# The projections of the mixing stage: plain fp32 products against three products of two-part operands

## The chip, the cores and the metric

One core of one Trainium2 chip runs the whole program: TensorE (PE in the profile) multiplies matrices, ScalarE (ACT), VectorE (DVE) and GpSimd (POOL) do the rest, and SyncE (SP) issues the weight loads. The metric is the time of one execution on the device in microseconds. The kernel before takes 1591.19 us, the median of three runs (1590.81 to 1591.87).

## The reference

Two transformer blocks on a sequence of 256 tokens with 1024 features, all in fp32. The change is in the mixing stage of the first block, behind its first feed-forward part:

```python
u = rms_norm(h, norm_mix)
proj = u @ w_in                       # [256 x 1024] @ [1024 x 4864]
aq, ak, av, rq, rf, ri, rg, ga, gb = jnp.split(proj, splits, axis=-1)
att = sliding_window_attention(aq, ak, av, rel_bias, attn_sinks)   # 8 heads of 64, window of 128
rec = hgrn2_recurrence(rq, rf, ri, lower_bounds)                   # 4 heads of 128
rec = rms_norm(rec, rec_norm) * sigmoid(rg)
merged = sigmoid(ga) * (att @ w_att_proj) + sigmoid(gb) * (rec @ w_rec_proj)
h = h + merged @ w_out
```

Only how `u @ w_in` is computed changes, and with it where its operands are kept.

## The kernel before

**Layout.** The features of `h` and of the scaled input `xT` lie on the partitions in eight tiles of 128, the 256 tokens along the row. `w_in` is cut into 19 chunks of 256 columns, 1 MB each. In the order of use they are `rf` (0, 1), `rq` (0, 1), `ri` (0, 1), `aq` (0, 1), `akv`, `rg` (0, 1) and `g` (0 to 7); below they are counted as chunks 0 to 18. All weights of the program pass through six bays of 1 MB. SyncE loads a chunk into its bay as soon as TensorE has used the chunk that lay there six places before (`load`, line 656).

**Products.** A chunk costs 16 matmuls of 128 x 128 by 128 x 256 (eight tiles of input features by two halves of the chunk), by `pair_of_features` (line 894, matmuls in `features`, line 808) or, for `ri`, `pair_of_tokens` (line 907). Plain fp32 matmuls stand in the trace as two records each. In `akv` the first half (keys) goes by features and the second (values) by tokens, with matmuls of 128 columns (line 975). The feed-forward parts already work in another way: ScalarE rounds a chunk into a first part in fp32r (line 1489), VectorE subtracts it from the raw chunk and writes the second part (line 2053), the input is split likewise, and TensorE sums first by first, second by first and first by second (`split_features`, lines 828 to 832): 48 matmuls to a chunk, each one record.

**Order.** Each engine runs its own list in the order in which it is written, and semaphores hold an instruction until what it needs is there. Around the change:
- TensorE (`mix1`, line 947): the embedding's product in four pieces (line 792), between them the sum of squares (line 744), the table of attention biases by distance (line 953) and the spread of the norm factors (line 780). Then chunks 0 to 10, the attention scores of eight heads (lines 991, 992), and a loop of nine steps over the levels of the recurrence: the level's scores (line 1013), then one of chunks 11 to 18.
- VectorE (line 2130): before the stage it adds the feed-forward result to `h` (line 2019) and folds squares (line 1983). Then it writes `xT` (line 2038), copies the bias table (line 2520), moves products out of PSUM, adds the biases to the scores (line 2160), and at each level multiplies (2190, 2191) and places masked scores (2184); behind level 3 it scales the probabilities (2232).
- ScalarE (line 1536): squares (1465), the embedding out of PSUM (1590), then `bias_out`: it issues a DMA that writes the bias table, copied 128 times, from eight partitions to a buffer in HBM (1534, 1.5 MB). After keeping `rf` it waits until that has landed and issues two loads that read it back shifted (1541, 1542). Then it keeps products (`keep`, line 1526) and takes exponentials (1557, 1561).
- GpSimd forms the differences of each level (1858, 1859).

## Time and profile before

| | |
|---|---|
| median of three runs | 1591.19 us |
| profiled execution | 1592.14 us, its span 1590.4 us |
| TensorE busy | 1499.5 us, 94% |
| VectorE, ScalarE, GpSimd busy | 832.7, 558.9, 152.0 us |
| mean granted TensorE clock | 0.956 of full speed |

The span runs from the first instruction to the last. The clock is the share of 2.4 GHz that TensorE was granted. The profile's times count from the span's start; the mixing stage runs from about 216 to 459 us, its projections from 227 to 385 us.

### The profile page before, as it was taken

How to read it: one execution, taken by the hardware profiler on the slowest of the kernel's cores; microseconds unless marked ns; L12 is line 12 of the kernel's file. 1: busy time of each engine (PE TensorE's matmuls, PEld its weight loads, DVE VectorE, ACT ScalarE, POOL GpSimd, SP SyncE). 2: the span in 40 equal slices, each digit the busy share in tenths (PEclk: the TensorE clock that was granted, in tenths of full speed). 3: DMA queues.
4: the chain of work that ended last, by engine and by line, in shares of the span. 5: the costliest groups of instructions: out<-in, count | busy, mean ns of one | idle time of the engine just before them, and what ended most of it. 6: DMA issues, size and time to landing. Idle time of an engine off the chain costs nothing.

```text
span 1590.4 us, 24781 instructions
## 1 busy us (share of the span) xinstructions
PE 1499.5 (94%) x10432; PEld 1398.4 (88%) x10432; DVE 832.7 (52%) x1130; ACT 558.9 (35%) x689; POOL 152.0 (10%) x149
## 2 busy tenths in 40 slices
PE   5999999899999999999979998999989889999997
PEld 5999998798899999988878878999988468999997
DVE  4666541253256565632664215766674263776765
ACT  3434321123035454421335103443442154444443
POOL 0000000121000000511020000000050032000023
PEclk8999999999999999999989759999999999999998
DMA  8555557533345555433400014455543312455530
GB/s 270 191 185 185 184 153 187 165 106 106 106 159 175 184 183 188 155 99 118 137 25 1 1 53 133 161 184 184 185 159 103 133 53 74 165 185 184 185 133 27
DMA packets 167213, 221.31 MB, mean 139 GB/s; under 512 B 5451, under 2 KB 148036, under 8 KB 167012
## 3 DMA queue, kind: packets, MB, share of 16 engines
q1 hardware_dynamic: 163564, 216.46, 41.2%
q10 hardware_dynamic: 3576, 3.81, 1.3%
q8 instruction: 55, 0.90, 0.2%
q14 instruction: 18, 0.15, 0.0%
HBM read 217.49 MB, written 2.62 MB: 138 GB/s over the span
## 4 chain that ended last, share of the span: by engine, by line
PE 85%; DVE 7%; ACT 4%; issue 2%; POOL 1%; DMA 0%; ACTq 0%; POOLq 0%; SPq 0%; DVEq 0%
PE ps L832 30%; PE ps L868 14%; PE ps L808 12%; PE ps L936 6%; PE ps L918 2%; PE ps L907 2%; PE ps L1231 1%; PE ps L792 1%; DVE x_second_part L1973 1%; PE ps L1352 1%; PE ps L818 1%; PE ps L1368 1%; PE ps L1013 1%; PE ps L1226 1%; PE ps L1380 1%
## 5 line engine op out<-in xcount | busy, mean ns | idle before, releaser
L2053 DVE TENSOR_TENSOR weights_second_parts<-weight_bays,weights_first_parts 128x2048 fp32r<-128x2048 f32 x132 | 302.9, 2302 | 173.5 <-ACT weights_first_parts L1489 173.2
L1489 ACT ACTIVATE weights_first_parts<-weight_bays 128x2048 fp32r<-128x2048 f32 x132 | 252.1, 1918 | 302.8 <-PE ps L832 191.4
L832 PE MATMUL ps<-x_first_part,weights_first_parts 128*128 128x256 f32 x1488 | 211.2, 285 | 1.7 <-DVE weights_second_parts L2053 1.7
L832 PE MATMUL ps<-x_second_part,weights_first_parts 128*128 128x256 f32 x1488 | 208.6, 283 | 0.0
L832 PE MATMUL ps<-x_first_part,weights_second_parts 128*128 128x256 f32 x1488 | 207.3, 282 | 0.0
L808 PE MATMUL ps<-xT,weight_bays 128*128 128x256 f32 (+1 forms) x896 | 197.4, 381 | 1.1 <-DVE xT L2038 1.1
L832 PEld LDWEIGHTS ps<-x_first_part,weights_first_parts 128*128 128x128 f32 x1488 | 192.6, 193 | 2.1 <-ACT weights_first_parts L1489 1.9
L832 PEld LDWEIGHTS ps<-x_second_part,weights_first_parts 128*128 128x128 f32 x1488 | 191.7, 191 | 0.0
L808 PEld LDWEIGHTS ps<-xT,weight_bays 128*128 128x128 f32 (+1 forms) x896 | 168.5, 189 | 26.1 <-ACT embedding L1597 1.3
L832 PEld LDWEIGHTS ps<-x_first_part,weights_second_parts 128*128 128x128 f32 x1488 | 190.6, 191 | 0.0
L868 PE MATMUL ps<-hidden_first_part,weights_first_parts 128*128 128x256 f32 x704 | 141.9, 283 | 5.4 <-ACT weights_first_parts L1489 3.7
L868 PE MATMUL ps<-hidden_second_part,weights_first_parts 128*128 128x256 f32 x704 | 141.9, 283 | 0.0
L868 PE MATMUL ps<-hidden_first_part,weights_second_parts 128*128 128x256 f32 x704 | 139.7, 279 | 0.0
L1868 POOL TENSOR_TENSOR weights_second_parts<-weight_bays,weights_first_parts 128x512 fp32r<-128x512 f32 x48 | 66.7, 1422 | 535.1 <-ACT weights_first_parts L1607 535.1
L868 PEld LDWEIGHTS ps<-hidden_first_part,weights_first_parts 128*128 128x128 f32 x704 | 107.7, 189 | 6.1 <-ACT weights_first_parts L1489 4.0
L868 PEld LDWEIGHTS ps<-hidden_second_part,weights_first_parts 128*128 128x128 f32 x704 | 109.1, 190 | 0.0
L868 PEld LDWEIGHTS ps<-hidden_first_part,weights_second_parts 128*128 128x128 f32 x704 | 108.8, 189 | 0.0
L936 PE MATMUL ps<-arena,weight_bays 128*128 128x256 f32 x320 | 71.6, 386 | 6.5 <-DVE arena L2406 4.5
L936 PEld LDWEIGHTS ps<-arena,weight_bays 128*128 128x128 f32 x320 | 61.7, 194 | 16.0 <-DVE arena L2406 4.7
L1842 POOL TENSOR_TENSOR rstd<-mean_squares,minus_half 128x2 f32<-128x2 f32 (+3 forms) x16 | 14.9, 934 | 562.5 <-DVE mean_squares L2025 426.2
L1526 ACT ACTIVATE arena<-ps 128x512 f32<-128x512 f32 x14 | 8.4, 597 | 121.5 <-PE ps L808 95.0
L1505 ACT ACTIVATE arena<-arena 128x512 f32<-128x512 f32 x22 | 13.9, 633 | 99.9 <-DVE arena L2072 99.9
(369 smaller groups left out, 1882.6 us busy)
## 6 DMA issues: line engine op xcount, KB each, us to landing
weight_bays<-in_w_ffn_in SPq DMA_DIRECT2D x44, 1024.0 KB, 5.2
weight_bays<-in_ffn_w_in SPq DMA_DIRECT2D x44, 1024.0 KB, 5.1
weight_bays<-in_w_ffn_out SPq DMA_DIRECT2D x22, 1024.0 KB, 4.9
weight_bays<-in_ffn_w_out SPq DMA_DIRECT2D x22, 1024.0 KB, 4.9
weight_bays<-in_w_in SPq DMA_DIRECT2D x19, 1024.0 KB, 5.5
weight_bays<-in_hyb_w_in SPq DMA_DIRECT2D x13, 1024.0 KB, 5.2
weight_bays<-in_ple_w_gate SPq DMA_DIRECT2D x8, 1024.0 KB, 4.9
weight_bays<-in_w_out SPq DMA_DIRECT2D x4, 1024.0 KB, 5.0
```

Of the source, the lines that this page charges most:

```text
L792: mm = nc.tensor.matmul(ps[:, b0 + q, j % 2 * SEQ:(j % 2 + 1) * SEQ], w[:, k, j * P:(j + 1) * P], pT[:, n, k], start=(k == 0), stop=(k == 1))
L808: mm = nc.tensor.matmul(dst, lhs(k), xT[:, k] if rhs is None else rhs(k), start=(k == 0), stop=(k == n - 1), **kw)
L818: nc.tensor.matmul(dst[j], w[:, k, j * P:(j + 1) * P], x_hi[:, k], start=(k == 0 and w is hi and not (one_bank and j)), stop=False, skip_g ...
L832: mm = nc.tensor.matmul(dst, w[:, k, j * P:(j + 1) * P], x[:, k], start=(n + k == 0), stop=(n == 2 and k == KD - 1))
L868: mm = nc.tensor.matmul(ps[:, tile // 2, tile % 2 * SEQ:(tile % 2 + 1) * SEQ], w[:, j, tile * P:(tile + 1) * P], x[:, g % 2, j], start=(g ...
L907: mm = nc.tensor.matmul(ps[:, b, t * width:(t + 1) * width], xT[:, k, t * P:(t + 1) * P], w[:, k, c0:c0 + width], start=(k == 0), stop=(k ...
L918: mm = nc.tensor.matmul(ps[:, b0 + j // 2, j % 2 * SEQ:(j % 2 + 1) * SEQ], w[k // 2][:, k % 2, j * P:(j + 1) * P], srcT[:, k], start=(k == ...
L936: mm = nc.tensor.matmul(ps[:, tile // 2, tile % 2 * SEQ:(tile % 2 + 1) * SEQ], w[:, j, tile * P:(tile + 1) * P], srcT(k) if callable(srcT) ...
L1013: mm = nc.tensor.matmul(o, a, c, start=True, stop=True)
L1489: nc.scalar.activation(hi, raw, ACT.Copy).then_inc(*w_hi_ready.inc(f, g, kind, of - g))
L1868: ins = nc.gpsimd.tensor_tensor(lo[:, part], raw[:, part], hi[:, part], ALU.subtract)
L2053: v.tensor_tensor(lo, raw, hi, ALU.subtract).then_inc(*w_lo_d.inc(f, g, kind, of - g))
```

## The change

Every chunk of `w_in` is split as in the feed-forward parts. ScalarE writes the first part (`prep`), VectorE the second (`rest_of_mix`), and TensorE runs 48 matmuls on them (`mix_features`, `mix_tokens`). First parts go to three slots in turn, and from chunk 13 on to two others (`late_hi`) in the place of the bias rows. The scaled input goes to the buffer `sq`, from there as first parts by ScalarE to `xT`'s place and as second parts by VectorE back into `sq`. All of `akv` goes by features now, and the values are turned by two transposes of TensorE. GpSimd's clearing of `AT` waits for the input's second parts.

```diff
+        mixer_lo = nc.alloc_sbuf_tensor_at("mixer_x_second_part", [P, KD, SEQ], F32R, offset=nc.sbuf_base - 4 * KD * SEQ)
         xT = sb("xT", [P, KD, SEQ])
+        mixer_hi = nc.alloc_sbuf_tensor_at("mixer_x_first_part", [P, KD, SEQ], F32R, offset=nc.sbuf_base - 4 * KD * SEQ)
...
+        late_hi, _ = carve_split(ARENA - 2 * BAY, "gate_weights_first_parts", 2, BAY)
...
+        MIX_SLOT = [n % 3 for n in range(12)] + [1]
+
+        def mix_views(m):
+
+            c = chunks[MIX_CHUNKS[m]] % BAYS
+            hi = w_hi[:, MIX_SLOT[m]] if m < len(MIX_SLOT) else late_hi[:, (m - len(MIX_SLOT)) % 2]
+            return [t.rearrange("p (a b) -> p a b", a=KD) for t in (bay[:, c], hi, bay_lo[:, c])]
...
+            mixer_x = (mixer_hi, mixer_lo)
+
+            def wait_mix(m):
+                pe.wait_ge(*w_hi_ready.at(MIX_CHUNKS[m]))
+                pe.wait_ge(*w_lo_d.at(MIX_CHUNKS[m]))
+                return mix_views(m)[1:]
+
+            def mix_features(m, b):
+
+                hi, lo = wait_mix(m)
+                if m == 0:
+                    mm = first_features("mix1", [ps[:, b, j * SEQ:(j + 1) * SEQ] for j in range(2)], hi, lo, True, mixer_x)
+                else:
+                    for j in range(2):
+                        mm = split_features(ps[:, b, j * SEQ:(j + 1) * SEQ], hi, lo, j, mixer_x)
+                through(mm, MIX_CHUNKS[m])
+            def mix_tokens(m, b):
+
+                hi, lo = wait_mix(m)
+                for t in range(TT):
+                    for n, (x, w) in enumerate(((mixer_hi, hi), (mixer_lo, hi), (mixer_hi, lo))):
+                        for k in range(KD):
+                            mm = nc.tensor.matmul(ps[:, b, t * SEQ:(t + 1) * SEQ], x[:, k, t * P:(t + 1) * P], w[:, k],
+                                                  start=(n + k == 0), stop=(n == 2 and k == KD - 1))
+                through(mm, MIX_CHUNKS[m])
...
-                pair_of_features(("rf", 0), 0, first="mix1")
-                pair_of_features(("rf", 1), 1)
-                pair_of_features(("rq", 0), 2)
+                mix_features(0, 0)
+                mix_features(1, 1)
+                mix_features(2, 2)
                 pe.wait_ge(*bias_d.at("t"))
-                pair_of_features(("rq", 1), 3)
+                mix_features(3, 3)
                 for n in range(2):
-                    weights(("ri", n))
                     pe.wait_ge(*proj_a.at("rf", n))
-                    through(pair_of_tokens(("ri", n), n), ("ri", n))
+                    mix_tokens(4 + n, n)
                 for n in range(2):
                     pe.wait_ge(*proj_d.at("rq", n))
-                    pair_of_features(("aq", n), 2 + n)
-                weights("akv")
+                    mix_features(6 + n, 2 + n)
                 pe.wait_ge(*proj_a.at("ri", 0))
...
+                mix_features(8, 0)
+                pe.wait_ge(*proj_a.at("ri", 1))
+                mix_features(9, 1)
+                pe.wait_ge(*proj_d.at("aq", 0))
+                mix_features(10, 2)
+
+                pe.wait_ge(*proj_d.at("akv"))
...
                 for t in range(TT):
+                    mm = nc.tensor.transpose(ps[:, 0, t * P:(t + 1) * P], vT[:, t * P:(t + 1) * P], ident)
+                mm.then_inc(*att_p.inc("v_turned"))
...
-                        pair_of_features(("g", n), pb)
+                        mix_features(11 + n, pb)
...
+            def prep(m):
+                raw, hi, _ = mix_views(m)
+                wait_weights(act, MIX_CHUNKS[m])
+                if m < 3:
+                    act.wait_ge(*used_up_to(("ffn1", 3 * GROUPS - 3 + m)))
+                elif m < len(MIX_SLOT):
+                    act.wait_ge(*used_up_to(MIX_CHUNKS[m - (3 if m < 12 else 2)]))
+                elif m < len(MIX_SLOT) + 2:
+                    act.wait_ge(*att_d.at("biased", AH - 1))
+                else:
+                    act.wait_ge(*used_up_to(MIX_CHUNKS[m - 2]))
+                nc.scalar.activation(hi, raw, ACT.Copy).then_inc(*w_hi_ready.inc(MIX_CHUNKS[m]))
+
             def mix1():
+                for q in range(PAIRS):
+                    act.wait_ge(*x_d.at("mix1", q))
+                    nc.scalar.activation(mixer_hi[:, 2 * q:2 * q + 2], sq[:, 2 * q:2 * q + 2], ACT.Copy).then_inc(*x_hi_a.inc("mix1", q))
+                bias_out()
                 for n in range(2):
+                    prep(2 + n)
                     keep(fT[:, 2 * n:2 * n + 2], n, ("rf", n), "rf", n, func=ACT.Sigmoid)
                 act.wait_ge(tab_out.sem, 16)
                 shifted = [bass.AP(tensor=scratch.tensor, offset=127 + o, ap=[[383, P], [384 * P, AH], [1, n]]) for o, n in ((0, 256), (P, P))]
                 act.dma_start(bias[:, :, 0:256], shifted[0]).then_inc(bias_in.sem, 16)
                 act.dma_start(bias[:, :, 256:384], shifted[1]).then_inc(bias_in.sem, 16)
+                prep(4)
+                prep(5)
                 for n in range(2):
+                    prep(6 + n)
                     keep(vR[:, :, n * 256:(n + 1) * 256], n, ("ri", n), "ri", n)
                 act.wait_ge(*rec_d.at("f"))
                 nc.scalar.activation(bT[:], fT[:], ACT.Ln).then_inc(*rec_a.inc("log"))
+                prep(8)
+                prep(9)
+                prep(10)
...
                 for n in range(2):
+                    prep(11 + n)
                     keep(sgT[:, 2 * n:2 * n + 2], 1 + n, ("rg", n), "rg", n)
 
                 act.wait_ge(*att_d.at("minus_max"))
...
                     act.wait_ge(*rec_g.at("differences", n))
                     nc.scalar.activation(zT[:, n % 2], zT[:, n % 2], ACT.Exp).then_inc(*rec_a.inc("decay", n))
                     keep(gT[:, 2 * n:2 * n + 2], (3 + n) % 4, ("g", n), "g", n)
+                    if n < 6:
+                        prep(13 + n)
...
+            prep(0)
+            prep(1)
             arrive("mix1")
             embedding("ple1", 4)
-            bias_out()
             mix1()
...
-                pool.wait_ge(*mean_ready.at("mix1"))
-                pool.wait_ge(*bias_p.at("t"))
+                pool.wait_ge(*x_lo_d.at("mix1", PAIRS - 1))
...
+            def rest_of_mix(m):
+                raw, hi, lo = mix_views(m)
+                dve.wait_ge(*w_hi_ready.at(MIX_CHUNKS[m]))
+                v.tensor_tensor(lo, raw, hi, ALU.subtract).then_inc(*w_lo_d.inc(MIX_CHUNKS[m]))
+
+            def split_x(n, gain, b):
+                dve.wait_ge(*spread_p.at(n))
+                for k in range(KD):
+                    ins = v.scalar_tensor_tensor(sq[:, k], h[:, k], gain(k), ps[:, b, 0:SEQ], ALU.mult, ALU.mult)
+                    if k % 2:
+                        ins.then_inc(*x_d.inc(n, k // 2))
+                for q in range(PAIRS):
+                    p = slice(2 * q, 2 * q + 2)
+                    dve.wait_ge(*x_hi_a.at(n, q))
+                    v.tensor_tensor(mixer_lo[:, p], sq[:, p], mixer_hi[:, p], ALU.subtract).then_inc(*x_lo_d.inc(n, q))
...
                 dve.wait_ge(*masks_ready.at())
                 for n in range(2):
+                    rest_of_mix(2 + n)
                     dve.wait_ge(*proj_a.at("rf", n))
                     if n == 0:
                         dve.wait_ge(*lb_d.at("one_minus"))
...
                 for n in range(2):
+                    rest_of_mix(4 + n)
                     keep(rqT[:, 2 * n:2 * n + 2], 2 + n, ("rq", n), "rq", n)
                 dve.wait_ge(*rec_d.at("f"))
                 v.tensor_scalar(kT[:], fT[:], -1.0, 1.0, ALU.mult, ALU.add).then_inc(*rec_d.inc("q_and_k"))
+                rest_of_mix(6)
+                rest_of_mix(7)
...
                 for n in range(2):
+                    rest_of_mix(8 + n)
                     keep(aqT[:, 2 * n:2 * n + 2], 2 + n, ("aq", n), "aq", n, scale=0.125)
                 dve.wait_ge(*rec_d.at("scan"))
                 v.tensor_copy(bT[:], fT[:]).then_inc(*rec_d.inc("sums"))
+                rest_of_mix(10)
                 dve.wait_ge(*used_up_to("akv"))
                 v.tensor_copy(akT[:, 0], ps[:, 0, 0:SEQ]).then_inc(*proj_d.inc("akT"))
...
-                keep(av[:], 0, "akv", "akv", c=slice(256, 512))
+                v.tensor_copy(vT, ps[:, 0, SEQ:2 * SEQ]).then_inc(*proj_d.inc("akv"))
+                rest_of_mix(11)
+                dve.wait_ge(*att_p.at("v_turned"))
+                v.tensor_copy(av[:], ps[:, 0, 0:SEQ].rearrange("p (a b) -> p a b", a=TT)).then_inc(*proj_d.inc("av"))
...
+                rest_of_mix(12)
...
                         normalize_probs()
+                    if n < 6:
+                        rest_of_mix(13 + n)
...
+            rest_of_mix(0)
+            rest_of_mix(1)
             arrive("mix1", added("ffn1", 0.5, ("ffn1", 3 * GROUPS - 1)))
             factors("mix1", b=0)
-            scaled_x("mix1", lambda k: col("norm_mix", k), 1)
+            split_x("mix1", lambda k: col("norm_mix", k), 1)
```

Three places show what this does to the order.

**ScalarE, from the last piece of the embedding to chunk 5.** L1534 is the write of the bias table, L1541 and L1542 the two loads that read it back, L1526 keeps a product. Before:

```order
L1590 ACTIVATE embedding<-ps 128x512 [waits weights_used]
L1530 ACTIVATE lower_bound<-lower_bound_logit 128x4 [waits lower_bound_by_vector]
L1534 DMA bias_by_distance<-arena 1024x1x384 [waits bias_by_distance_copied]
L1526 ACTIVATE arena<-ps 128x512 [waits weights_used] x2
L1541 DMA arena<-bias_by_distance 128x8x256 [waits bias_by_distance_stored]
L1542 DMA arena<-bias_by_distance 128x8x128
L1526 ACTIVATE arena<-ps 128x2x256 [waits weights_used] x2
```

Now (L1571, L1596, L1597 are the same three DMAs, L1563 keeps a product, L1584 writes the first part of a chunk, L1589 that of the input):

```order
L1654 ACTIVATE embedding<-ps 128x512 [waits weights_used]
L1589 ACTIVATE mixer_x_first_part<-squares 128x512 [waits xT_by_vector] x4
L1567 ACTIVATE lower_bound<-lower_bound_logit 128x4 [waits lower_bound_by_vector]
L1571 DMA bias_by_distance<-arena 1024x1x384 [waits bias_by_distance_copied]
L1584 ACTIVATE weights_first_parts<-weight_bays 128x2048 [waits weights_used,weights_landed0]
L1563 ACTIVATE arena<-ps 128x512 [waits weights_used]
L1584 ACTIVATE weights_first_parts<-weight_bays 128x2048 [waits weights_used,weights_landed1]
L1563 ACTIVATE arena<-ps 128x512 [waits weights_used]
L1596 DMA arena<-bias_by_distance 128x8x256 [waits bias_by_distance_stored]
L1597 DMA arena<-bias_by_distance 128x8x128
L1584 ACTIVATE weights_first_parts<-weight_bays 128x2048 [waits weights_used,weights_landed2]
L1584 ACTIVATE weights_first_parts<-weight_bays 128x2048 [waits weights_used,weights_landed3]
```

Four input parts stand ahead of the write, the first parts of chunks 2 and 3 ahead of the two loads, and the first parts of chunks 4 and 5 behind them.

**VectorE, at the end of the feed-forward part.** L2019 adds the result to `h`, L1983 folds squares. Before:

```order
L1968 TENSOR_TENSOR one_and_squared_gain<-vector_columns 128x8
L2019 SCALAR_TENSOR_TENSOR h<-ps,h 128x512 [waits projection_ready] x3
L2019 SCALAR_TENSOR_TENSOR h<-ps,h 128x512 [waits weights_used]
L1983 TENSOR_TENSOR squares<-squares 128x512 [waits squares_summed]
L1983 TENSOR_TENSOR squares<-squares 128x512 [waits vector_step,squares_summed]
L2025 TENSOR_SCALAR mean_squares<-ps 128x2 [waits squares_added]
```

Now, with L2109 as the second part of a weight chunk, L2083 and L2047 for L2019 and L1983:

```order
L2032 TENSOR_TENSOR one_and_squared_gain<-vector_columns 128x8
L2109 TENSOR_TENSOR weights_second_parts<-weight_bays,weights_first_parts 128x2048 [waits weights_first_part_ready] x2
L2083 SCALAR_TENSOR_TENSOR h<-ps,h 128x512 [waits projection_ready] x3
L2083 SCALAR_TENSOR_TENSOR h<-ps,h 128x512 [waits weights_used]
L2047 TENSOR_TENSOR squares<-squares 128x512 [waits squares_summed]
L2047 TENSOR_TENSOR squares<-squares 128x512 [waits vector_step,squares_summed]
L2089 TENSOR_SCALAR mean_squares<-ps 128x2 [waits squares_added]
```

The second parts of chunks 0 and 1 stand ahead of the four updates of `h`.

**VectorE, two levels of the recurrence.** L2190 and L2191 multiply, L2184 places scores under a mask. Before:

```order
L2190 TENSOR_TENSOR arena<-arena 128x256x2 [waits recurrence_by_scalar]
L2191 TENSOR_TENSOR arena<-arena 128x256x2
L2184 COPY_PREDICATED arena<-masks,ps 128x512 [waits recurrence_by_vector,recurrence_by_tensor]
L2184 COPY_PREDICATED arena<-masks,ps 128x512
L2190 TENSOR_TENSOR arena<-arena 128x128x4 [waits recurrence_by_scalar]
L2191 TENSOR_TENSOR arena<-arena 128x128x4
L2184 COPY_PREDICATED arena<-masks,ps 128x512 [waits recurrence_by_vector,recurrence_by_tensor]
L2184 COPY_PREDICATED arena<-masks,ps 128x512
```

Now (L2280, L2281 and L2274 are the same three lines):

```order
L2109 TENSOR_TENSOR weights_second_parts<-weight_bays,gate_weights_first_parts 128x2048 [waits weights_first_part_ready]
L2280 TENSOR_TENSOR arena<-arena 128x256x2 [waits recurrence_by_scalar]
L2281 TENSOR_TENSOR arena<-arena 128x256x2
L2274 COPY_PREDICATED arena<-masks,ps 128x512 [waits recurrence_by_vector,recurrence_by_tensor]
L2274 COPY_PREDICATED arena<-masks,ps 128x512
L2109 TENSOR_TENSOR weights_second_parts<-weight_bays,gate_weights_first_parts 128x2048 [waits weights_first_part_ready]
L2280 TENSOR_TENSOR arena<-arena 128x128x4 [waits recurrence_by_scalar]
L2281 TENSOR_TENSOR arena<-arena 128x128x4
L2274 COPY_PREDICATED arena<-masks,ps 128x512 [waits recurrence_by_vector,recurrence_by_tensor]
L2274 COPY_PREDICATED arena<-masks,ps 128x512
L2109 TENSOR_TENSOR weights_second_parts<-weight_bays,gate_weights_first_parts 128x2048 [waits weights_first_part_ready]
```

Before each level's two products now stands the second part of a gate chunk.

## Rows read from the trace of the kernel before

**Rows 1.** The page, part 1: busy us (share) and instructions of each engine
```profile
PE 1499.5 (94%) x10432; PEld 1398.4 (88%) x10432; DVE 832.7 (52%) x1130; ACT 558.9 (35%) x689; POOL 152.0 (10%) x149
```

**Rows 2.** The chain of waits in order of time: start us, us, what
```profile
54.79 11.40 PE ps L832 x96
...
219.27 1.68 PE ps L744 x16
...
227.45 27.63 PE ps L808 x128
255.08 13.81 PE ps L907 x64
268.89 17.27 PE ps L808 x80
286.16 3.57 PE ps L975 x32
...
316.68 7.70 PE ps L808 x32
324.38 1.78 PE ps L1013 x16
```

**Rows 3.** The page, part 5: splitting a chunk; busy us, mean ns of one, idle before
```profile
L2053 DVE TENSOR_TENSOR weights_second_parts<-weight_bays,weights_first_parts 128x2048 fp32r<-128x2048 f32 x132 | 302.9, 2302 | 173.5 <-ACT weights_first_parts L1489 173.2
L1489 ACT ACTIVATE weights_first_parts<-weight_bays 128x2048 fp32r<-128x2048 f32 x132 | 252.1, 1918 | 302.8 <-PE ps L832 191.4
```

**Rows 4.** Timeline of ScalarE, stage entry: start us, us, instruction, idle before it
```profile
209.74 1.08 ACT L1782 ACTIVATE pT<-ps 128x512 f32<-128x512 f32 x2 [3.32 <-PE ps L729]
...
227.49 0.60 ACT L1590 ACTIVATE embedding<-ps 128x512 f32<-128x512 f32 x1 [2.37 <-PE ps L792]
...
229.16 0.84 ACTq L1534 DMA_DIRECT2D bias_by_distance<-arena  x1
...
264.69 0.42 ACTq L1541 DMA_DIRECT2D arena<-bias_by_distance  x1
...
265.78 0.60 ACT L1526 ACTIVATE arena<-ps 128x512 f32<-128x512 f32 x1 [23.88 <-issue]
```

**Rows 5.** Timeline of VectorE, stage entry
```profile
215.85 0.69 DVE L2019 SCALAR_TENSOR_TENSOR h<-ps,h 128x512 f32<-128x512 f32 x1 [0.72 <-PE ps L868]
216.46 1.48 DVE L1983 TENSOR_TENSOR squares<-squares 128x512 f32<-128x512 f32 x2
...
228.59 0.54 DVE L2520 COPY arena<-ps 8x384 f32<-8x384 f32 x1
```

**Rows 6.** DMA queues, 243 to 246 us (two rows), then 246 to 249 us (two rows)
```profile
q1 hardware_dynamic: 499, 0.50, 48.6%
q10 hardware_dynamic: 93, 0.14, 45.1%
...
q10 hardware_dynamic: 94, 0.14, 45.6%
q1 hardware_dynamic: 1, 0.00, 0.0%
```

**Rows 7.** Busy time by stretch: PE, PEld, DVE, ACT, POOL, PEclk, DMA share, GB/s
```profile
312.90:318.10 5.20, 5.20 (x20) 4.92 (x21) 1.11 (x5) 3.95 (x18) 0.00 (x0) 0.50 0.02 3
```

**Rows 8.** Timeline, the recurrence's levels: VectorE and GpSimd
```profile
322.96 0.69 DVE L2191 TENSOR_TENSOR arena<-arena 128x512 f32<-128x512 f32 x1
...
326.60 1.53 DVE L2191 TENSOR_TENSOR arena<-arena 128x512 f32<-128x512 f32 x1
328.05 1.33 DVE L2184 COPY_PREDICATED arena<-masks,ps 128x512 f32<-128x512 uint8 x2
...
347.14 3.76 DVE L2232 TENSOR_SCALAR arena<-arena,softmax_sum 128x256 f32<-128x256 f32 x16
...
326.24 1.33 POOL L1858 TENSOR_TENSOR arena<-arena 128x512 f32<-128x512 f32 x1 [38.09 <-PE ps L1013]
```

**Rows 9.** Timeline of ScalarE, an exponential of the recurrence
```profile
324.91 1.05 ACT L1561 ACTIVATE arena<-arena 128x1024 f32<-128x1024 f32 x1
```

More of the change, by code:

```diff
@@ L389, in build @@
         sgT, at = carve(at, RH, SEQ)
+        akT, at = carve(at, 2, SEQ)
         gT, at = carve(at, 16, SEQ)
@@ L438, in build @@
         block_out = signal("first_block_out")
+        MIX_CHUNKS = [("rf", 0), ("rf", 1), ("rq", 0), ("rq", 1), ("ri", 0), ("ri", 1), ("aq", 0), ("aq", 1), "akv", ("rg", 0), ("rg", 1),
+                      *[("g", n) for n in range(8)]]
+        MIX_SLOT = [n % 3 for n in range(12)] + [1]
[3 more added lines that the diff above has]
+            return [t.rearrange("p (a b) -> p a b", a=KD) for t in (bay[:, c], hi, bay_lo[:, c])]
         def ple_views(key):
@@ L809, in features, with first_features @@
                 return mm
-            def first_features(f, dst, hi, lo, one_bank):
+            def first_features(f, dst, hi, lo, one_bank, xs=(x_hi, x_lo)):
                 for q in range(PAIRS):
@@ L1019, in mix1 @@
                         elif n == 1:
-                            pe.wait_ge(*proj_d.at("akv"))
+                            pe.wait_ge(*proj_d.at("av"))
                         elif n < 4:
```

20 lines of the change are left out of this document (5 added, 15 removed).

## The prediction

> **What bounds the kernel now.** I read the page first. TensorE is busy for 94% of the span [rows 1], so what its own work costs counts nearly in full, unless something new makes it wait. The chain of waits in order of time comes next: from 227.45 us on it holds nothing but projection matmuls, one chunk behind the other, until the attention scores [rows 2]. VectorE and ScalarE have idle time there. So the question is in two parts: what a chunk costs TensorE in either form, and whether the two helpers deliver the parts in time. For the second I read the timelines of ScalarE and VectorE from the end of the feed-forward part on, each against the new order of instructions.
>
> **A chunk on TensorE.** Plain fp32: 27.63 us for 128 records, which are four chunks, so 6.91 us each. Two-part: 11.40 us for 96 matmuls of the same shape, which are two chunks of the feed-forward part, so 5.70 us each [rows 2]. That is 1.21 us less per chunk. `akv` costs 3.57 us for the values and two tenths of the 17.27 us for half a chunk by features (80 records are five halves, 3.45 each), 7.02 in all; now 5.70, 1.32 less. The two transposes of the values add 0.5 us (a level's 16 records of 128 columns take 1.78 us [rows 2], four such records 0.45). With TensorE never waiting, 18 x 1.21 + 1.32 - 0.5 = 22.6 us would be gained.
>
> **Stage entry.** ScalarE is done with `pT` at 209.74 + 1.08 = 210.82 [rows 4] and now writes two first parts, 1.92 us each [rows 3]: 212.74 and 214.66. VectorE's second parts take 2.30 each [rows 3] and end at 215.04 and 217.34. Only then come the four updates of `h`, the last of which started at 215.85 before. They follow each other at 0.61 us (215.85 to 216.46 [rows 5]), so the last starts at 219.2, the squares at 219.8 and end 1.48 later, at 221.2. TensorE began the sum at 219.27 [rows 2]: it is 1.9 us late, and so is the end of the embedding, 229.4 instead of 227.45. ScalarE then takes the last piece of the embedding out of PSUM (0.60 [rows 4]) before it rounds the first pair of `x`, a copy of the same size. TensorE starts chunk 0 at 230.6 and is done with chunk 3 at 230.6 + 4 x 5.70 = 253.4 us. The parts of chunks 2 and 3 are there by then: each needs 4.2 us of the two helpers, and TensorE has work for 11.4 us before chunk 2.
>
> **The wait for the bias table.** This decides. In the new order ScalarE writes the first parts of chunks 4 and 5 only behind the two loads of the bias, and these wait until the table's write to HBM has landed. Before, the write was issued at 229.16 and ScalarE got past that wait at 264.69, 35.5 us later [rows 4]. It cost nothing then: behind it stood only the keeping of `ri`, done at 261.99, and TensorE went on with raw chunks. Now TensorE needs chunk 4's parts. The write itself is issued later: the four copies of `x` end at 232.4, VectorE's last second part takes about 0.7 us (to 233.1), the copy of the table 0.54 [rows 5] with a small one ahead of it, so the write starts at 233.8. I keep 35.5 us for it: 269.3. The two loads are issued within 1.1 us (264.69 to 265.78 [rows 4]), the first part takes 1.92, the second 2.30: chunk 4 starts at 274.6, where it started at 255.08 [rows 2]. TensorE stands for 21.2 us and is **19.5 us late**. VectorE is in the same jam: its second part of chunk 4 stands ahead of `rq`'s keeping, which chunk 6 waits for, but it has 11 us for that..
>
> **From there to the end of the stage** come 15 chunks, 14 x 1.21 + 1.32 = **-18.3 us**, and the transposes, **+0.5**. In these 15 the helpers mostly keep up. A gate round costs TensorE 1.78 + 5.70 = 7.48 us. ScalarE has 0.60 + 1.92 + 1.05 in it [rows 3, 4, 9]. VectorE has the second part 2.30, two products (0.69 each, one of them 1.53 while GpSimd works) and the placing 1.33 [rows 3, 8]: 5.0 to 5.9. Two places are tight. The first level's products ended at 323.65 [rows 8], 0.7 us ahead of the end of the gate chunk at 324.38 [rows 2], which now comes 1.2 earlier: 0.5 us of wait. And behind level 3 VectorE has the 3.8 us of the probabilities [rows 8] in one round, 9.2 to 9.6 in all against 7.48, of which about 1.5 is slack: 0.4 us more. Together **+0.9**; the bounds are 0 and 4.
>
> **The clock.** After TensorE stood for 3.5 us ahead of 312.89, its granted clock was 0.50 for the next 5.2 us, the 1.2 GHz level [rows 7], and a chunk there took 7.70 us instead of 6.91 [rows 2]. Half of 5.2 is 2.6 us. The new wait of 21 us is longer than that one, and I price what follows it the same, **+2.6**. It can be no gain; the bounds are 0 and twice the row, 5.2. The old wait ahead of the first level stays and is counted already.
>
> **Sum.** 19.5 - 18.3 + 0.5 + 0.9 + 2.6 = +5.2 us on the profiled execution's 1592.14 us (span 1590.4 and 1.7 around it), 1597.3. That execution lay 0.95 above the median of the runs, so I forecast 1596 for the median, with some tenths off for instructions that overlap by 0.08 where I added full durations. Behind the stage nothing changes: later loads have room, since TensorE's wait only fills the bays.
>
> **The rule on the write.** The rows: in 243 to 246 us the write (q10) moved 93 packets beside 499 of the weight loads (q1), in 246 to 249 it moved 94 beside one [rows 6], both at 45% of the 16 DMA engines. So its speed doesn't depend on the weight loads, and the long stop of these doesn't shorten it. The Trainium skill, "DMA: Bandwidth & Descriptors", section "Why a DMA increments its semaphore by 16 and not by 1", says that a DMA uses the largest number of engines up to 16 that divides the outer sizes of both sides. The write reads eight partitions: eight engines, and 45% agrees. The same page, "Queues, rings and completion order", has each engine take turns between the queues that have work. By that rule the write would get the engines whole once TensorE stops and no load is left; the trace disagrees. It is the ground of the first rival.
>
> **Rivals.**
> - *Faster, the write lands earlier.* Place: ScalarE's wait for the table. If the weight loads did share the write's engines and their stop halved its 35.5 us, it would land at 251.6. Chunk 4 would start at 256.9, 1.8 us late instead of 19.5, with a short wait and no cold clock: 1596 - 17.7 - 2.6 = 1576. The change gains from the point where the write is over 5 us shorter, and by over 0.2% from 8.4 us. For it: loads and write do run side by side. Against it: rows 6, and that few loads are under way in the write's second half already. 12%, all shortenings together.
> - *No difference.* The wait is as forecast, but the clock comes back sooner or the entry and the gate rounds lose nothing: 19.5 - 18.3 + 0.5 + 1 = +2.7, 1594. 20%.
> - *VectorE bounds the gate rounds.* GpSimd's differences run beside it, and a product of 0.69 took 1.53 meanwhile [rows 8]. If the second parts stretched in the same proportion, 2.30 to 5.1, a round would be 8.7 us against TensorE's 7.48, and six rounds would lose 1.2 each: 1603. Against it: the stalled product lost 0.84 us, about what was left of one GpSimd instruction of 1.33, which looks like waiting once and not like half speed. The Trainium skill, "GPSIMD Engine Reference", "Specifications", says that the two engines contend where VectorE reads two inputs from SBUF, as the second parts do; it gives no price. 8%.
> - *The two-part chunks don't cost 5.70.* The input's parts lie elsewhere and `ri` has them as the stationary side, but shape and type are those of the row. If they cost 6.3, 15 x 0.6 = 9 us more, 1605. 2%.
>
> **Chances and range.** The forecast holds 58%. What a measurement can tell from no change is 0.2%, 3.2 us, so faster is below 1588 and slower above 1594.4. Faster 0.12, same 0.20, slower 0.68 (58 + 8 + 2). The forecast's own range is 1594.5 to 1601. With the second rival and part of the third it is 1590 to 1602; the faster case is left out.
>
> **What would show it.** ScalarE: idle for about 27 us ahead of the first load of the bias, at 269. TensorE: one idle stretch of about 21 us behind the fourth chunk, ended by the second part of chunk 4, with the granted clock at 0.50 for some microseconds behind it; 48 matmuls in 5.70 us everywhere else; gate rounds of 7.5 us. The level scores behind the last gate chunk at 390 us instead of 385. Wrong it would be if ScalarE passed the wait before 260, if TensorE's stretch were under 15 us, or if gate rounds took 8 us or more.

## The result, and the profile after

The changed kernel takes 1599.9 us, the median of 14 runs (1595.4 to 1602.44); the kernel before, run beside it on the same chips, 1588.11 (14 runs, 1584.38 to 1592.24). The ratio is 1.0063, with a 95% interval of 1.0049 to 1.0077: slower, by 8 to 12 us. The profiled execution took 1596.38 us, its span 1594.4.

The executions of either kernel fall mostly into two groups some 6 us apart (the kernel before: seven of 1584.38 to 1585.41 us and seven of 1590.81 to 1592.24, with the median between them), and since the profiled execution of before (1592.14) is of the upper group and that of after (1596.38) by its time of the lower, the 4 us between their spans are not the cost of the change. The cost is read from the ratio, and from the stage itself. From the start of the embedding's product to the start of the attention's output projection it took 402.23 - 215.65 = 186.58 us before and 412.00 - 215.10 = 196.90 after: +10.3 us, in line with the ratio (0.63% of 1588 is 10.0). All stage times below are read this way. A second execution of the kernel before (experiment 9) has 184.68, which would make it +12.2: stages of single executions can be compared to within some 2 us, and what a smaller difference means has to be read from the rows.

The page, part 1, answers to [rows 1]:

```profile
PE 1476.2 (93%) x10722; PEld 1388.0 (87%) x10722; DVE 877.8 (55%) x1154; ACT 595.4 (37%) x712; POOL 160.9 (10%) x149
```

TensorE is busy for 23 us less than before and the program is slower all the same: it stands more. The waits of TensorE between 215 and 412 us say where (line of the waiting matmul, what it waits for, us in total, times, longest):

```profile
PE ps L939 <- DVE weights_second_parts L2109: 21.0, 1, 21.0
PE ps L1050 <- DVE arena L2281: 4.0, 2, 2.7
PE ps L1050 <- DVE arena L2249: 3.5, 1, 3.5
PE ps L758 <- DVE squares L2047: 1.7, 1, 1.7
PE ps L1092 <- ACT arena L1644: 1.7, 1, 1.7
PE ps L832 <- ACT mixer_x_first_part L1589: 1.3, 1, 1.3
```

The third and the fifth row stood before too (3.5 and 1.7). The other four are new. The first is the forecast's main term. The chain of waits in order of time (start us, us, what), answering to [rows 2]:

```profile
220.45 2.62 PE ps L758 x16
...
234.99 35.06 DMA bias_by_distance<-arena
270.53 0.59 ACTq L1597
271.22 1.92 ACT weights_first_parts L1584
273.16 2.30 DVE weights_second_parts L2109
275.60 13.34 PE ps L939 x96
288.94 28.33 PE ps L846 x240
...
337.67 2.05 PE ps L1050 x16
339.72 5.67 PE ps L846 x48
...
370.76 2.88 PE ps L1050 x16
373.65 6.38 PE ps L846 x48
380.03 1.78 PE ps L1050 x16
381.81 5.69 PE ps L846 x48
```

The write of the bias table is now a link of the chain, 35.06 us long; where it stood beside the chain before, TensorE now waits for ScalarE's first part behind it and VectorE's second. A chunk costs 5.67 us (28.33 for five of 48 matmuls), as forecast. ScalarE's timeline answers to [rows 4]:

```profile
234.99 0.84 ACTq L1571 DMA_DIRECT2D bias_by_distance<-arena  x1
...
270.07 0.42 ACTq L1596 DMA_DIRECT2D arena<-bias_by_distance  x1
270.53 0.59 ACTq L1597 DMA_DIRECT2D arena<-bias_by_distance  x1
271.22 5.51 ACT L1584 ACTIVATE weights_first_parts<-weight_bays 128x2048 fp32r<-128x2048 f32 x3 [27.27 <-issue]
```

Between the write and the loads ScalarE is idle for the longer part, 27 us, and three first parts follow in a row behind it. The granted clock (column behind POOL) in three half-speed stretches that are new or longer than before, answering to [rows 7]:

```profile
221.50:228.30 6.80, 6.80 (x21) 4.79 (x21) 0.64 (x3) 0.11 (x1) 0.70 (x1) 0.50 0.00 0
259.10:279.60 20.50, 4.00 (x19) 4.03 (x20) 6.44 (x6) 5.51 (x3) 0.00 (x0) 0.50 0.82 220
371.70:375.10 3.40, 3.40 (x18) 3.40 (x17) 3.40 (x4) 0.00 (x0) 1.37 (x1) 0.50 0.20 80
```

Each lies in or behind one of the new waits. Before, the profiled execution had 3.4 us at half speed at the first place and none at the other two.

VectorE's timeline in the gate rounds, answering to [rows 8]:

```profile
355.33 2.74 DVE L2109 TENSOR_TENSOR weights_second_parts<-weight_bays,gate_weights_first_parts 128x2048 fp32r<-128x2048 f32 x1 [1.44 <-ACT gate_weights_first_parts L1584]
357.99 1.60 DVE L2280 TENSOR_TENSOR arena<-arena 128x512 f32<-128x512 f32 x1
...
361.82 5.39 DVE L2324 TENSOR_SCALAR arena<-arena,softmax_sum 128x256 f32<-128x256 f32 x16
```

The probabilities take 5.39 us instead of 3.76, a second part 2.74 instead of 2.30. GpSimd at the same time (its rows are rough):

```profile
354.87 1.05 POOL L1922 TENSOR_TENSOR arena<-arena 128x512 f32<-128x512 f32 x1 [3.40 <-PE ps L1050]
355.88 3.17 POOL L1923 TENSOR_TENSOR arena<-arena 128x512 f32<-128x512 f32 x1
```

### The profile page after: what moved, and what is told of

It is laid out like the page before. It is cut to its first block, busy times and chain, and to the rows that moved or that the text cites. A ratio compares the mean times of both kernels' runs of the same rounds, so it can differ in the third digit from the quotient of the medians.

```text
span 1594.4 us, 25429 instructions
## 1 busy us (share of the span) xinstructions
PE 1476.2 (93%) x10722; PEld 1388.0 (87%) x10722; DVE 877.8 (55%) x1154; ACT 595.4 (37%) x712; POOL 160.9 (10%) x149
## 4 chain that ended last, share of the span: by engine, by line
PE 79%; DVE 10%; ACT 4%; DMA 3%; issue 2%; POOL 1%; ACTq 0%; POOLq 0%; SPq 0%; DVEq 0%
PE ps L846 33%; PE ps L882 14%; PE ps L977 5%; PE ps L822 5%; DMA bias_by_distance<-arena 2%; PE ps L959 2%; PE ps L1268 1%; DVE x_second_part L2037 1%; PE ps L1389 1%; PE ps L1405 1%; PE ps L832 1%; PE ps L1263 1%; PE ps L806 1%; PE ps L948 1%; PE ps L1417 1%
## 5 line engine op out<-in xcount | busy, mean ns | idle before, releaser
L2133 DVE TENSOR_TENSOR weights_second_parts<-weight_bays,weights_first_parts 128x2048 fp32r<-128x2048 f32 x132 | 301.1, 2289 | 172.0 <-ACT weights_first_parts L1526 171.6
L1526 ACT ACTIVATE weights_first_parts<-weight_bays 128x2048 fp32r<-128x2048 f32 x132 | 252.1, 1918 | 299.5 <-PE ps L846 190.1
L822 PE MATMUL ps<-xT,weight_bays 128*128 128x256 f32 (+1 forms) x368 | 80.8, 380 | 1.1 <-DVE xT L2102 1.1
L822 PEld LDWEIGHTS ps<-xT,weight_bays 128*128 128x128 f32 (+1 forms) x368 | 68.2, 186 | 12.7 <-ACT embedding L1661 1.3
L2109 DVE TENSOR_TENSOR weights_second_parts<-weight_bays,weights_first_parts 128x2048 fp32r<-128x2048 f32 x13 | 29.9, 2307 | 42.6 <-ACT weights_first_parts L1584 42.6
L1542 ACT ACTIVATE arena<-arena 128x512 f32<-128x512 f32 x22 | 13.9, 633 | 99.9 <-DVE arena L2152 99.9
```

Of the source, the lines that this page charges most:

```text
L822: mm = nc.tensor.matmul(dst, lhs(k), xT[:, k] if rhs is None else rhs(k), start=(k == 0), stop=(k == n - 1), **kw)
L1526: nc.scalar.activation(hi, raw, ACT.Copy).then_inc(*w_hi_ready.inc(f, g, kind, of - g))
L2109: v.tensor_tensor(lo, raw, hi, ALU.subtract).then_inc(*w_lo_d.inc(MIX_CHUNKS[m]))
L2133: v.tensor_tensor(lo, raw, hi, ALU.subtract).then_inc(*w_lo_d.inc(f, g, kind, of - g))
```

## The experiments

There are nine experiments. Their stage times (before 186.6, after 196.9) come from one profiled execution each, the ratios from timed runs against the kernel before.

**1. The wait for the table behind the second `ri` piece.**

```diff
-                act.wait_ge(tab_out.sem, 16)
-                shifted = [bass.AP(tensor=scratch.tensor, offset=127 + o, ap=[[383, P], [384 * P, AH], [1, n]]) for o, n in ((0, 256), (P, P))]
-                act.dma_start(bias[:, :, 0:256], shifted[0]).then_inc(bias_in.sem, 16)
-                act.dma_start(bias[:, :, 256:384], shifted[1]).then_inc(bias_in.sem, 16)
                 prep(4)
                 prep(5)
                 for n in range(2):
                     prep(6 + n)
                     keep(vR[:, :, n * 256:(n + 1) * 256], n, ("ri", n), "ri", n)
+                act.wait_ge(tab_out.sem, 16)
...
```

> The changed kernel with ScalarE's wait for the bias table and the two loads behind it moved from ahead of the first parts of chunks 4 and 5 to behind the keeping of ri. The stage is measured from the start of the embedding's product to the start of the first output projection: 186.6 us in the kernel before, 196.9 in the changed one. Theory 1 (the write stands in ScalarE's queue and besides holds the weight loads issued while it runs): chunks 4 and 5 start without a wait at 254 and 260 us, and TensorE then stands about 8 us for chunk 6, whose load lands only with the write's end near 270 us; the stage takes 182 to 184 us, some 14 less than in the changed kernel. Rival (the loads are not held, only ScalarE's queue was): no wait of TensorE before the attention scores, the stage takes 173 to 175 us. Rival 2 (TensorE's wait had another cause): 196 to 197 us as before.

Measured: 1591.16 us, ratio 1.0007 (0.999 to 1.0024); stage 186.1. The wait ahead of chunk 4 is gone, and with it the loss: the position of that wait is what made the change slower. But 8.3 us came back ahead of chunk 6. The stage is above the 182 to 184 expected, since that wait had half clock behind it too (30.87 us for chunks 6 to 10 instead of 28.33) and the stretch at half clock in the gate rounds was 6.8 us long instead of 3.4. The chain shows from where the 8.3 us come:

```profile
237.77 32.19 DMA weight_bays<-in_w_in
...
269.98 1.92 ACT weights_first_parts L1584
...
271.92 2.31 DVE weights_second_parts L2109
...
274.36 30.87 PE ps L846 x240
```

A weight load of 1 MB, issued at 237.77 while the write of the table was under way, landed 32.19 us later, when the write was done. So the write holds up TensorE in two ways: through ScalarE's wait, and, once that is gone, through the weight loads beside it.

**2. The probabilities three rounds later.** They are wanted only behind the last gate chunk.

```diff
-                    if n == 3:
+                    if n == 6:
                         normalize_probs()
```

> The changed kernel with the scaling of the probabilities moved on VectorE from behind level 3 to behind level 6, nothing else. Theory (the scaling, 5.4 us beside GpSimd's differences, makes the products of level 4 late): TensorE's wait of 2.7 us ahead of level 5 and the 1.8 us of half clock behind it go, stage 192.0 to 193.0 us instead of 196.9. Rival (VectorE's total work per round is the bound): the wait only moves to a later level, stage above 195.5.

Measured: 1593.52 us in one run; stage 192.5, 4.4 less. The wait of 2.7 us at 370.8 is gone, and so is the half-speed stretch behind it; that at 338 stays with 1.1. The theory holds: the scaling was what made TensorE wait. Of these 4.4 us the prediction had 0.4.

**3. The table written 32 times instead of 128.** The loads then read it in four groups of 32 partitions; what arrives in the bias rows is the same.

```diff
-                act.dma_start(scratch, tabd[:].unsqueeze(1).to_broadcast([AH, P, 384])).then_inc(tab_out.sem, 16)
+                act.dma_start(scratch[:, 0:32], tabd[:].unsqueeze(1).to_broadcast([AH, 32, 384])).then_inc(tab_out.sem, 16)
...
+                for r in range(0, P, 32):
+                    for c, o, n in ((0, 0, 256), (256, P, P)):
+                        src = bass.AP(tensor=scratch.tensor, offset=127 + o - r, ap=[[383, 32], [384 * P, AH], [1, n]])
+                        act.dma_start(bias[r:r + 32, :, c:c + n], src).then_inc(bias_in.sem, 16)
```

> The changed kernel, with the bias table written to HBM 32 times instead of 128, and read back in four groups of 32 partitions (eight loads instead of two, the same bytes read and the same values). Theory (the length of the write sets the wait, 35.1 us at 128 copies): the write lands about 10 us after its issue, near 245 us; with some 4 us for issuing eight loads chunk 4's parts are ready at 254, when TensorE comes for them; its 21.0 us of waiting and the 1.9 us of half clock behind it go, the stage takes 173.5 to 175.5 us, and the kernel 21 to 23 us less than the changed one. Rival (the write's time is mostly a fixed cost of its landing, not of its bytes): the write still takes over 25 us and the gain is under 10 us. The gate rounds keep their waits of 4.0 us in sum.

Measured: 1580.75 us, ratio 0.9938 (0.9915 to 0.9962); stage 175.6. The write was issued at 234.91 and ScalarE passed the wait at 244.28, 9.4 us later. So the write's time goes with its bytes, and the rival is refuted. TensorE goes from chunk 3 to chunk 4 with no wait, and chunk 6 doesn't wait either:

```profile
249.97 4.60 PE ps L846 x39
254.58 11.52 PE ps L939 x96
266.10 28.33 PE ps L846 x240
```

With the write out of the way the stage is 11 us shorter than before, though the entry and the gate rounds still lose what they lost.

**4. The same 32 copies in the kernel before**, to see whether the write alone is worth something.

> The kernel before with the same 32 copies and eight loads, its products unchanged. Theory (the write cost nothing there, since raw chunks 4 and 5 were in their bays and ScalarE's lateness held nobody): no difference, stage 186.3 to 187.0 us, ratio within 0.2% of 1. Rival (the write's slowing of the weight loads already cost the kernel before something): 1 to 3 us faster.

Measured: 1591.09 us, ratio 0.9997 (0.998 to 1.0014); stage 186.5. The write was free there, to within what the interval leaves open. It is the change that put a price on it.

**5. The entry: the second parts of chunks 0 and 1 behind the updates of `h`.**

```diff
-            rest_of_mix(0)
-            rest_of_mix(1)
             arrive("mix1", added("ffn1", 0.5, ("ffn1", 3 * GROUPS - 1)))
+            rest_of_mix(0)
             factors("mix1", b=0)
             split_x("mix1", lambda k: col("norm_mix", k), 1)
+            rest_of_mix(1)
```

> The changed kernel with VectorE's second parts of chunks 0 and 1 behind the four updates of h (chunk 0's ahead of the norm factors, chunk 1's behind the second parts of x), nothing else. Theory (those two hold the updates of h, and with them the sum of squares, the factors, x and the write of the bias table): TensorE's wait of 1.7 us ahead of the sum goes, chunk 0 starts 2 to 5 us earlier, the write is issued as much earlier, and chunk 4, which waits for it, too: stage 192 to 195 us instead of 196.9. Rival (the entry is hidden in the 21 us of waiting): stage unchanged at 196.9, since TensorE only waits longer.

Measured: 1597.96 us in one run; stage 194.7, 2.2 less. Chunk 0 started 3.5 us earlier (228.24 instead of 231.78), but chunk 4 only 1.0 earlier, at 274.56: TensorE now stood 23.4 us ahead of it instead of 21.0. The write went out at 233.65, only 1.3 us earlier, since the second part of chunk 1 (2.28 us from 230.80 on) now stands ahead of the table's copy on VectorE. So most of what the entry gained was waited away, and of the 1.0 us another 0.4 went in chunks 4 and 5, which took 13.79 us instead of 13.34. The rival is nearly right. The rest of the 2.2 us, 1.6, lies in the gate rounds: in this execution the wait of 2.7 us, which is still there, has no stretch at half clock behind it. The edit does not touch that place, so I don't count these 1.6 us for it.

**6. All of 2, 3 and 5.**

> The changed kernel with three edits: 32 copies as in the run before; the second parts of chunks 0 and 1 behind the updates of h (one ahead of the factors, one behind the second parts of x); and the scaling of the probabilities moved from behind level 3 to behind level 6. Theory: to the 23 us of the shorter write come 1.7 us of wait and about 3 us of half clock and later start at the entry, and 2.7 us of wait and 1.8 of half clock at level 5; the stage takes 165 to 168 us, 19 to 21 us less than in the kernel before, and the whole about 1.2% less than before. Rival (VectorE's total work bounds the gate rounds, wherever the scaling stands): the 4.5 us of the gate rounds stay, stage 170 us or more.

Measured: 1574.79 us, ratio 0.9907 (0.9883 to 0.9931); stage 172.7, above the 165 to 168 expected. TensorE stood for 5.1 us ahead of chunk 4. ScalarE was past the wait at 243.2, so it wasn't the write:

```profile
243.21 8.80 ACTq L1598 DMA_DIRECT2D arena<-bias_by_distance  x8
252.12 5.51 ACT L1584 ACTIVATE weights_first_parts<-weight_bays 128x2048 fp32r<-128x2048 f32 x3 [11.46 <-PE ps L846]
```

ScalarE issued the eight loads for 8.8 us, ahead of the first part of chunk 4. (In experiment 3 the same eight took 5.75, and TensorE came 3 us later.) The first six went out in 2.8 us, the last two took 2.74 and 3.18; what held these is not shown.

**7. As 6, with the first parts of chunks 4 and 5 ahead of the eight loads.**

```diff
+                prep(4)
+                prep(5)
                 act.wait_ge(tab_out.sem, 16)
                 for r in range(0, P, 32):
...
-                prep(4)
-                prep(5)
```

> All edits of the run with 32 copies, the early entry and the late probabilities, and in addition ScalarE makes the first parts of chunks 4 and 5 ahead of the wait for the bias table and of its eight loads, which it issues behind them. Theory: the 5.1 us that TensorE still stood ahead of chunk 4 there was ScalarE's 8.8 us of issuing loads between 243.2 and 252.1, ahead of the first part of chunk 4, and not the write, which had landed by 243.2; then chunk 4 starts behind chunk 3 at about 251.4 with no wait, the loads go out at 247 to 256, chunk 6 (read from 262.8) has its first part by 258.3 and its second by 261, so no wait takes its place, and the stage falls from 172.7 to 167 to 168 us, the time from 1574.8 to about 1570. Rival: the weights' second parts by VectorE bound chunk 4 by themselves; then the wait stays at 3 us or more and the stage stays at 171 us or above. Second rival: the eight issues push a wait of 3 to 5 us to chunk 6, and the stage stays within 1 us of 172.7.

Measured: **1568.97 us** (1564.96 to 1571.11), ratio 0.9868 (0.9847 to 0.9889), the best of all and better than either kernel; stage 165.9. The first theory holds: no wait ahead of chunk 4, none ahead of chunk 6. The stage fell by 6.8 us, more than expected: the wait of 5.1, and 1.6 of half clock behind it (chunks 4 and 5 take 11.32 us instead of 12.95). The chain from the embedding's end:

```profile
228.04 3.97 PE ps L832 x32
232.01 1.89 PE ps L838 x16
233.90 17.00 PE ps L846 x144
250.91 11.32 PE ps L939 x96
262.23 28.33 PE ps L846 x240
```

It is TensorE alone from chunk 0 to the attention scores, 11 chunks of 5.7 us.

**8. GpSimd nearly idle beside two rounds.** Most of the differences of two levels are left out.

```diff
+                    few = slice(None) if n not in (4, 5) else slice(0, 1)
-                    nc.gpsimd.tensor_tensor(z[:, :, 0:m], mid, b[:, :, 0:m], ALU.subtract)
-                    nc.gpsimd.tensor_tensor(z[:, :, m:2 * m], b[:, :, m:2 * m], mid, ALU.subtract)...
+                    nc.gpsimd.tensor_tensor(z[:, few, 0:m], mid[:, few], b[:, few, 0:m], ALU.subtract)
+                    nc.gpsimd.tensor_tensor(z[:, few, m:2 * m], b[:, few, m:2 * m], mid[:, few], ALU.subtract)...
```

> The changed kernel, but of GpSimd's differences for two of the levels (the fifth and the sixth of its eight, at 354.9 and 362.4 us) only the first block is worked out, so that GpSimd is idle there; this leaves most of these differences out of the computation. All other instructions, waits and their order stay, and the differences ahead of them (at 339.8 and 347.3) stay as they were: they are the control. Theory: VectorE is slowed by GpSimd's instructions beside it. Then the second part at 355.3 takes 2.3 us instead of 2.74 and the product at 358.0 takes 0.69 instead of 1.60, while in the control round 347.9 stays at 2.59 and 350.4 at 1.64; the 16 instructions of the probabilities start 1.4 us earlier and take 3.4 to 3.8 us instead of 5.39; the wait of 2.72 us at 370.8 falls to 0 or under 0.3, and with the 1.8 us of half clock behind it the stage falls from 196.9 by 2.7 to 4.5 us. Rival: the durations are VectorE's own (the operands' places, or its waits for the last write); then they stay as they are, and the wait stays at 2.7 us.

Measured: 1593.33 us in one run; stage 194.0, 2.9 less. VectorE, the control round (first two rows) and the round with GpSimd idle:

```profile
348.04 2.58 DVE L2110 TENSOR_TENSOR weights_second_parts<-weight_bays,gate_weights_first_parts 128x2048 fp32r<-128x2048 f32 x1 [2.19 <-ACT gate_weights_first_parts L1584]
350.55 1.65 DVE L2281 TENSOR_TENSOR arena<-arena 128x512 f32<-128x512 f32 x1
...
355.50 2.29 DVE L2110 TENSOR_TENSOR weights_second_parts<-weight_bays,gate_weights_first_parts 128x2048 fp32r<-128x2048 f32 x1 [1.45 <-ACT gate_weights_first_parts L1584]
357.71 0.68 DVE L2281 TENSOR_TENSOR arena<-arena 128x512 f32<-128x512 f32 x1
...
360.64 3.88 DVE L2325 TENSOR_SCALAR arena<-arena,softmax_sum 128x256 f32<-128x256 f32 x16
```

2.74 became 2.29, 1.60 became 0.68, 5.39 became 3.88, the control stayed, and the wait of 2.7 us was gone. VectorE and GpSimd do slow each other here. This execution has a stretch at half clock from 399.4 to 402.8 us, behind the last level, that the changed kernel's lacks and that costs 1.5 us; without it the stage would be 4.4 us shorter than 196.9, as in experiment 2. The Trainium skill, "GPSIMD Engine Reference", "Specifications", names "contention with DVE instructions in a 2-port perf mode or with two SBUF inputs" (DVE is VectorE). The second part and the product have two inputs from SBUF, and for them the runs agree. The scalings have one tensor input and a scalar per partition, and they were slowed as well; whether they ran in such a mode no run here shows.

**9. The kernel before, once more**, for the profile of an execution of the lower group.

> The kernel before once more, unchanged, for a second trace. Its runs lie in two groups about 6.5 us apart (1584.5 and 1591), those of the changed kernel too (1595.6 and 1602). The first trace of the kernel before is of the upper group, that of the changed kernel of the lower. Theory: the two groups differ in a stage that the change does not touch, by the granted clock; a trace of the lower group would have the mixing stage at 186.6 us and be shorter in the second block's first mixing part, between 790 and 970 us. If this run is of the upper group again, its trace should repeat the first.

Measured: 1584.45 us, span 1582.7; stage 184.7, where the other execution had 186.6. The theory that the groups differ only elsewhere was wrong: 1.9 us lie in the stage, 1.5 at its entry and 0.4 at the first level. At the entry 2.80 us for eight matmuls of L792 in one trace stand beside 1.93 in the other:

```profile
221.97 1.93 PE ps L792 x8
223.90 0.62 PE ps L780 x4
224.52 1.73 PE ps L792 x8
```

The upper group's execution has 3.4 us at half clock there, this one none. It also lacks the stretches at 14, 663 and 687 us; without the last two it gains 3.2 us. What decides into which group an execution falls stays open.

## Why the prediction was right, and where it wasn't

The sign, the place and the mechanism were right, and the measured median lies in the range. The size was not: the sum said +5.2 us, the stage shows +10.3. That 1599.9 us fell into 1594.5 to 1601 was in part luck. The kernel before came out at 1588.11, 3.1 us below the 1591.19 that I had started from, and this hid part of the 5.1 us by which the sum was short; +10.3 on 1591.19 would have been 1601.5.

- **A chunk, -1.21.** Right: 5.67 to 5.70 us against 6.91. Experiment 3 shows the products' gain nearly bare, 11.0 us with the losses of the entry and the gate rounds still in it.
- **The wait for the table.** Right as a mechanism and nearly in size. Write 35.06 (35.5 kept from before), TensorE idle 20.95 (forecast 21.2), chunk 4 at 275.60 (274.6). Counted from the embedding's start, which came 0.55 us earlier, it is 21.1 us late instead of 19.5. Experiments 1 and 3 take the wait and the write away, and the loss goes with either.
- **The entry, mis-sized by 1.7 us.** The order of events was right: the sum of squares began at 220.45, 1.7 us of idle ahead of it and 1.9 us late. The step "it is 1.9 us late, and so is the end of the embedding" failed. Behind this wait the clock was at half for 6.8 us instead of 3.4, which costs 1.7 more: from the start of the sum to the end of the embedding it took 10.0 us (220.45 to 230.49) where it had taken 8.35 (219.10 to 227.45). The five traces with this wait (after, experiments 1, 2, 3 and 8) all have 6.8 us at half clock there, the six without it 3.4 or, in experiment 9, none. I had priced the clock behind the long wait only.
- **The gate rounds, mis-sized by 3.1 us.** The two places were right, the first level's products (1.25 us) and level 3's probabilities (2.72); the sum was 4.0 instead of +0.9. At the first level 0.7 of the 1.25 is no loss: TensorE was through with the chunk that much sooner, since it spent only 4.0 us of the old half-clock stretch at work instead of 5.3. At level 3 the failed step is "9.2 to 9.6 in all against 7.48": the round took VectorE 11.8 us (355.33 to 367.13). Beside GpSimd the probabilities cost 5.39 and not 3.8 and the second part 2.74 and not 2.30, and the two small instructions ahead of the probabilities, 0.5 us, were not in the sum. I had read 1.53 beside 0.69 as one instruction that waits once; experiment 8 shows that the second parts and the probabilities are slowed too. The third rival had the mechanism, but at double durations throughout; the second parts took at most 2.74, not 5.1. One sign of being wrong, "gate rounds took 8 us or more", did come: the round ahead of the wait of 2.72 took 10.4 us with it, and the next, at half clock, 9.1. The other rounds behind the first took 7.5 to 7.6. The level scores behind the last gate chunk came at 394.85, not at 390.
- **The clock, +2.6.** At chunk 4 it was 1.9 (13.34 us for two chunks of 5.70). Two further pieces, 1.7 us at the entry and 1.8 in the gate rounds, make 5.4; the 0.7 saved at the first level leave 4.7, within the bounds of 0 and 5.2. In this trace the waits of 1.7, 21 and 2.7 us had such a stretch in or behind them, and the one of 1.25 had none. A wait doesn't fix its length: the one of 2.7 us had 3.4 us here, 6.8 in experiments 1 and 3 and none in experiment 5.
- Sum of the misses: 1.6 (chunk 4 later) + 3.1 (waits in the gate rounds) + 1.8 (clock in the gate rounds) - 0.7 (clock at chunk 4) - 0.7 (clock at the first level) - 0.5 (chunks at 5.67) = 4.6, of the 5.1 that were short. The rest lies in small pieces, such as level scores of 2.05 us instead of 1.78 behind a wait.
- **The first rival, a shorter write,** is refuted: 35.06 us. But the sentence on the rule, "the trace disagrees", went too far. The DMA queues from 258 to 261 us after:

```profile
q10 hardware_dynamic: 89, 0.14, 42.3%
q1 hardware_dynamic: 91, 0.09, 8.7%
```

  Between 252 and 265 us the weight loads get about as many packets through as the write, in three windows of 3 us 75, 91 and 94 beside 90, 89 and 96. That fits the taking of turns that the Trainium skill describes ("DMA: Bandwidth & Descriptors", "Queues, rings and completion order"). In the window above the two queues together keep only 51% of the 16 engines busy, as if what is left of the loads stood behind the write on its eight; which engine moved which packet these rows don't show. The write keeps its pace, which was 95 packets with no loads beside it (249 to 252 us), and the loads are slow: experiment 1 has one of 32.19 us. The same could be read in the trace of the kernel before, from 255 to 258 us:

```profile
q10 hardware_dynamic: 88, 0.14, 41.9%
q1 hardware_dynamic: 91, 0.09, 8.7%
```

  Its weight loads issued beside the write took 24 to 31 us, against 5.3 for the one ahead of it, so "few loads are under way in the write's second half" was wrong as well. I asked the rule only what the loads do to the write and not what the write does to the loads.
- **Behind the stage nothing changes:** as far as the traces show. The distance between the two profiled executions is +9.8 us until 790 us and some +5.0 from 1028 on, with the difference in half-speed stretches between 800 and 1011. The two executions of the kernel before move against each other by as much, 5.3 us between 655 and 1028, so I don't count it for the change.

## What to carry to other kernels

When an engine that ran beside the critical path becomes a supplier of the bound engine, walk its list for waits that were free, and look for the long transfer behind each: here one wait on a DMA turned a change worth -11 us into +10. Moving the wait only undid the loss (stage 186.1 against 186.6), because the transfer then held the weight loads; shortening the transfer gave the gain back (175.6). Price each new idle stretch of TensorE twice, once as a wait and once as the half clock that may follow it. Look at what a slow transfer does to the loads beside it, and at the time to issue a DMA that was split into many. And before a difference of 2 us between two single executions is put down to an edit, see whether their half-clock stretches are the same.

## What the runs showed of the hardware

- A write of 1.5 MB from eight partitions took 34.8 to 35.5 us, one of 0.375 MB 9.4. Weight loads of 1 MB issued beside the long one took 24 to 33 us (in the kernel before, the changed one and experiment 1), beside the short one or the eight loads behind it 9 to 16 (experiments 3 and 7), ahead of the write 5 to 7.
- ScalarE needed 8.8 us to issue eight loads in experiment 6 and 4.5 to 5.8 in experiments 3, 4 and 7.
- VectorE beside GpSimd: a product of 0.68 us took 1.53 to 1.77, a second part of 2.29 up to 2.79, 16 scalings of 3.9 took 5.39; GpSimd's own instruction of 1.04 took up to 3.2.
- Two executions of the kernel before, 1592.14 and 1584.45 us, differ in part by stretches at half clock that the one has and the other lacks.
